# Moving the activation buffers by 32 bytes, and summing the norms' totals in two rounded halves

## The reference

```python
def rmsnorm_2(x, g):
    y = xf * lax.rsqrt(jnp.mean(xf * xf, axis=-1, keepdims=True) + EPS)
...
h = rmsnorm(x, norm_mix_g[layer])          # layer 0: RWKV time mix; layer 1: conformer convolution
x = x + memory_cross_attention(rmsnorm(x, norm_xattn_g[layer]), memn, ...)
x = x + conv_ffn(rmsnorm(x, norm_ffn_g[layer]), ffn_w_in[layer], ffn_dw[layer], ffn_w_out[layer])
...
# then one hybrid layer: gated linear attention + forgetting attention on rmsnorm_2(x) @ w_in,
# an output projection, and a feed-forward with 2 x 2816 inner features
```

## Time and profile before

| | |
|---|---|
| median of 3 runs | 2613.34 us (2609.92 to 2617.4) |
| span of the profiled execution | 2609.5 us |
| PE busy | 2513.7 us, 96% of the span |
| PEld busy | 2370.4 us, 91% |
| DVE, ACT, POOL busy | 1338.1, 1120.9, 995.1 us |
| matmuls at L565 (the dense products) | about 17,800 |

### The profile page before, as it was taken

How to read it: one execution, slowest core, us unless ns; L and a number is a source line. 1 busy time by engine, 2 the same in 40 slices (tenths; PEclk the granted TensorE clock), 3 DMA queues, 4 the chain that set the end, 5 groups by cost and what they waited for, 6 DMA issues and landing times.

```text
span 2609.5 us, 62290 instructions
## 1 busy us (share of the span) xinstructions
PE 2513.7 (96%) x25298; PEld 2370.4 (91%) x25298; DVE 1338.1 (51%) x2034; ACT 1120.9 (43%) x1649; POOL 995.1 (38%) x488
## 2 busy tenths in 40 slices
PE   6999898999999999998999999999999999999998
PEld 6888896897999999977989999999999769999998
DVE  7657554613477741798534777621153344455521
ACT  7844455544434433334534334433244443444432
POOL 3324220461444444325323444444442104444442
PEclk8899999999999999999999999999999999999999
DMA  4221001251222232313211222233222102222232
GB/s 147 74 65 58 2 1 63 94 181 41 89 96 96 88 101 101 130 65 105 89 65 65 97 96 96 97 105 113 89 89 74 41 1 94 97 92 96 94 100 73
DMA packets 62180, 219.43 MB, mean 84 GB/s; under 512 B 6752, under 2 KB 9184, under 8 KB 61408
## 3 DMA queue, kind: packets, MB, share of 16 engines
q1 hardware_dynamic: 58880, 207.76, 23.8%
q10 hardware_dynamic: 3168, 9.75, 1.1%
HBM read 213.29 MB, written 4.19 MB: 83 GB/s over the span
## 4 chain that ended last, share of the span: by engine, by line
PE 83%; DVE 8%; issue 6%; ACT 2%; POOL 1%; DMA 0%; DVEq 0%; POOLq 0%; ACTq 0%
PE psum L565 70%; DVE psum L2685 5%; PE psum L707 3%; PE psum L715 2%; PE psum L1066 1%; PE psum L1015 1%; PE psum L1245 1%; PE psum L1246 1%; POOL wl L514 1%; PE psum L1281 1%; DVE psum L2254 1%; ACT wh L1373 0%; PE psum L677 0%; PE psum L1269 0%; PE psum L684 0%
## 5 line engine op out<-in xcount | busy, mean ns | idle before, releaser
L514 POOL TENSOR_TENSOR wl<-raw,wh 128x1024 fp32r<-128x1024 f32 x388 | 949.0, 2456 | 1472.2 <-ACT wh L1373 1472.1
L565 PE MATMUL psum<-acth,wh 128*128 128x256 f32 x3792 | 763.4, 283 | 21.0 <-DVE actl L2776 8.2
L565 PE MATMUL psum<-actl,wh 128*128 128x256 f32 x3792 | 753.1, 280 | 0.0
L565 PE MATMUL psum<-acth,wl 128*128 128x256 f32 x3792 | 753.0, 280 | 0.0
L1373 ACT ACTIVATE wh<-raw 128x1024 fp32r<-128x1024 f32 x388 | 407.0, 1056 | 628.4 <-PE psum L565 610.9
L565 PEld LDWEIGHTS psum<-acth,wh 128*128 128x128 f32 x3792 | 582.1, 189 | 38.6 <-issue 30.4
L565 PEld LDWEIGHTS psum<-acth,wl 128*128 128x128 f32 x3792 | 581.0, 189 | 0.0
L565 PEld LDWEIGHTS psum<-actl,wh 128*128 128x128 f32 x3792 | 580.3, 189 | 0.0
L2615 DVE TENSOR_TENSOR cu<-psum,rstd 128x512 f32<-128x512 f32 x132 | 91.0, 689 | 241.7 <-PE psum L565 224.8
L565 PE MATMUL psum<-hidh,wh 128*128 128x256 f32 x1056 | 209.6, 276 | 0.0
L565 PE MATMUL psum<-hidh,wl 128*128 128x256 f32 x1056 | 209.3, 276 | 0.0
(11 more groups left out here) (436 smaller groups left out, 4044.3 us busy)
## 6 DMA issues: line engine op xcount, KB each, us to landing
raw<-in_weights SPq DMA_DIRECT2D x388, 512.0 KB, 3.3
xt<-in_x SPq DMA_DIRECT2D x4, 512.0 KB, 5.6
xt<-in_x ACTq DMA_DIRECT2D x1, 2048.0 KB, 9.2
out_x<-xt SPq DMA_DIRECT2D x6, 256.0 KB, 2.3
mem<-in_mem ACTq DMA_DIRECT2D x1, 1024.0 KB, 11.0
memn<-memh ACTq DMA_DIRECT2D x1, 1024.0 KB, 5.4
memn<-meml ACTq DMA_DIRECT2D x1, 1024.0 KB, 9.3
memh<-memn ACTq DMA_DIRECT2D x1, 1024.0 KB, 4.7
```

The source lines that it names most:

```text
L514: pool.tensor_tensor(wl[:, s, :], raw[:, s, :], wh[:, s, :].bitcast(F32), ALU.subtract).then_inc(split_done, 1)
L565: ins = pe.matmul(out[:, n:n + HALF], w, m[:, n:n + HALF], start=first and n == 0, stop=last and n + HALF >= out.shape[1])
```

## The change

1. `acth` is moved up by 32 bytes, so `acth` and `actl` begin 64 bytes beyond a multiple of 128. The small buffers behind are reordered so that `zone` stays where it was. The squares' buffer `sq` now begins 96 bytes beyond a multiple of 128, that is 32 beyond a multiple of 64.
2. Of a norm's sum ACT writes a rounded copy (`sum_high`, into `sums`, which lies on `sq`), DVE the rest (`sum_low`), and `norm_total` takes both with a rounded matrix of ones in matmuls of 256 columns: four for 512 tokens, two for 256. The first norm, the layer norm (`exact_total`) and `acc_x` in `in2` keep the float32 matmul.
3. `norm_total` stands one tile later in `up0`, `up1`, `up2`, `cin`, `in2`, `q1` and `o`; in `kv0` it stays. Loops are cut differently to suit.

```diff
         xt = place("xt", [P, KT, T + 1])
+        cursor[0] += 32
         act_at = cursor[0]
+        assert act_at % P == 64
...
-        common = place("common", [P, 3 * P])
+        par = place("par", [P, NPAR + 6])
+        sq = place("sq", [P, 2, T])
+        sums = at("sums", [P, 2, T], F32R, sq_at)
+        common = place("common", [P, 2 * P])
+        ones_r = place("ones", [P, P], F32R)
+        assert zone % 512 == 192 and sq_at % 64 == 32
...
+            def norm_total(stage, n=T, to=4):
+                pe.wait_ge(sum_lo, plan(stage, "sums") + 1)
+                for j in range(2):
+                    for c in range(0, n, HALF):
+                        ins = pe.matmul(bank[to][:, c:c + HALF], ones_r[:, :], sums[:, j, c:c + HALF], start=j == 0 and c == 0,
+                                        stop=j == 1 and c + HALF >= n)
+                ins.then_inc(sum_mm, 1)
...
                 tile("o", j, "post", acth, actl)
-                if j == 1:
+                if j == 2:
                     norm_total("norm_mem0", MEM)
...
             def ffn(l):
                 up, norm = f"up{l}", f"norm_ffn{l}"
                 tile(up, 0, norm, acth, actl)
+                tile(up, 1, norm, acth, actl)
                 norm_total(norm)
-                dense(up, norm, acth, actl, units=2 * FT - 4, skip=1)
+                dense(up, norm, acth, actl, units=2 * FT - 4, skip=2)
...
                 tile("cin", 0, "norm_conv", acth, actl)
+                tile("cin", 1, "norm_conv", acth, actl)
                 norm_total("norm_conv")
...
                 pe.matmul(bank[4][:, :], ones, acc_x[:, :], start=True, stop=True)
-                pe.matmul(bank[5][:, :], ones, acc_y[:, :], start=True, stop=True).then_inc(sum_mm, 1)
+                norm_total("norm_h", to=5)
...
+            def sum_high(stage, n=T):
+                act.wait_ge(sq_used, plan(stage, "sq") + KT + SC)
+                act.activation(sums[:, 0, 0:n], rstd[:, 0:n], ACT.Identity).then_inc(sum_hi, 1)
...
+            def sum_low(stage, n=T, of=rstd):
+                dve.wait_ge(sum_hi, plan(stage, "sums") + 1)
+                dve.tensor_tensor(sums[:, 1, 0:n], of[:, 0:n], sums[:, 0, 0:n].bitcast(F32), sub).then_inc(sum_lo, 1)
```

More of the change, by code:

```diff
@@ L165, in norm @@
         n = KT if split else 0
-        self.take(stage, sq=KT, rstd=1, split=n, val=n)
+        self.take(stage, sq=KT, rstd=1, split=n, val=n, sums=n // KT)
     def __call__(self, stage, what):
@@ L208, in build_program @@
         plan.take(f"down{l}", tile=8, x=KT)
-    plan.take("norm_h", sq=2 * KT, rstd=1, split=KT, val=KT, total=1)
+    plan.take("norm_h", sq=2 * KT, rstd=1, split=KT, val=KT, total=1, sums=1)
     plan.take("final", x=KT)
@@ L261, in build_program @@
         zone = cursor[0]
[L262 removed]
+        ident, blk64 = (common[:, j * P:(j + 1) * P] for j in range(2))
+        ones = ones_r[:, :].bitcast(F32)
+        assert zone % 512 == 192 and sq_at % 64 == 32
         b_eps, b_ln, b_gn, b_rn, b_q, b_eps2 = (eps[:, j:j + 1] for j in range(6))
@@ L603, in tile, with exact_total @@
                 ins.then_inc(units_used, 1)
-            def norm_total(stage, n=T):
+            def exact_total(stage):
                 pe.wait_ge(sq_used, plan(stage, "sq") + KT + SC)
-                pe.matmul(bank[4][:, 0:n], ones, rstd[:, 0:n], start=True, stop=True).then_inc(sum_mm, 1)
+                pe.matmul(bank[4][:, :], ones, rstd[:, :], start=True, stop=True).then_inc(sum_mm, 1)
+            def norm_total(stage, n=T, to=4):
[5 more added lines that the diff above has]
+                ins.then_inc(sum_mm, 1)
             def down(stage, source, hi, lo):
@@ L633, in _ @@
             pe.wait_ge(common_in, 16)
-            norm_total("norm0")
+            pe.wait_ge(ones_ready, 1)
+            exact_total("norm0")
             for b in (1, 2):
-                pe.matmul(bank[b][:, 0:3 * P], ones, common[:, :], start=True, stop=True)
-                pe.matmul(bank[b][:, 3 * P:T], ones, ident, start=True, stop=True)
+                for c in range(0, T, HALF):
+                    pe.matmul(bank[b][:, c:c + HALF], ones, common[:, :], start=c == 0, stop=c > 0)
             def mixed(stage, j, name):
@@ L1035, in attention @@
                     tile("q1", 0, "norm_x1", headh, headl)
+                    tile("q1", 1, "norm_x1", headh, headl)
                     pe.wait_ge(vt_ready, 8)
                     norm_total("norm_x1")
-                    dense("q1", "norm_x1", headh, headl, units=4, skip=1)
+                    for j in range(2, 5):
+                        tile("q1", j, "norm_x1", headh, headl)
                     pe.wait_ge(evacuated, plan("q1", "tile") + 2 + UC)
@@ L1099, in convolution @@
                 tile("cin", 0, "norm_conv", acth, actl)
+                tile("cin", 1, "norm_conv", acth, actl)
                 norm_total("norm_conv")
-                dense("cin", "norm_conv", acth, actl, units=4, skip=1)
-                for j in range(5, 8):
+                dense("cin", "norm_conv", acth, actl, units=4, skip=2)
+                for j in range(6, 8):
                     tile("cin", j, "norm_conv", acth, actl)
@@ L1123, in hybrid @@
                 tile("in2", 0, "norm_h", acth, actl)
+                tile("in2", 1, "norm_h", acth, actl)
                 pe.wait_ge(acc_ready, 1)
                 pe.matmul(bank[4][:, :], ones, acc_x[:, :], start=True, stop=True)
-                pe.matmul(bank[5][:, :], ones, acc_y[:, :], start=True, stop=True).then_inc(sum_mm, 1)
+                norm_total("norm_h", to=5)
                 def inner(skip, n):
                     dense("in2", "norm_h", acth, actl, units=n, skip=skip)
-                inner(1, 12)
+                inner(2, 8)
+                for j in range(10, 13):
+                    tile("in2", j, "norm_h", acth, actl)
                 pe.wait_ge(evacuated, t0 + 13 + UC)
@@ L1477, in deltas_normed @@
                         weight_high(UNIT0[stage] + (s + 1) * per - 1 + SLOTS, i, 4 * per)
+                if not gain:
+                    sum_high(norm)
             def last_deltas():
@@ L1955, in hybrid @@
             def hybrid():
+                act.wait_ge(acc_ready, 1)
+                act.activation(sums[:, 0, :], acc_y[:, :], ACT.Identity).then_inc(sum_hi, 1)
                 act.wait_ge(x_ready, plan("down1", "x") + KT + SC)
@@ L2207, in residual_normed @@
                             dve.tensor_tensor(b[:, :], b[:, :], sq[:, (n * s + j) % 2, :], add).then_inc(sq_used, 1)
+                if n == 1:
+                    sum_low(norm)
             def residual_last():
@@ L2651, in ffn @@
                                              op0=mul, op1=add).then_inc(acc_ready, 1)
+                    sum_low("norm_h", of=acc_y)
                 else:
```

24 lines of the change are left out of this document (14 added, 10 removed).

## The result

The changed kernel takes **2641.09 us** (median of four runs, 2640.94 to 2643.21) against 2611.63 us for the kernel before on the same chip: ratio 1.0115, 95% interval 1.0101 to 1.0129. It is slower by 1.2%, where 2581 us was forecast. The profiled execution has a span of 2639.1 us.

A forecast was written before the change was run, and what follows sets the result against it. PE's pace through the dense products was taken to bound the kernel. Pace -34.3, totals -1.6, `cin` +2.9, `o`/`kv0` +1.2 give -31.8 us: 2577.7 us span, plus 3.8 for the median, forecast 2581 us, range 2570 to 2602.

The forecast's parts named there:

- the three paces: Dense products: 113.2 ns on buffers 64 bytes beyond a multiple of 128, 116.6 on `acth`/`actl`, 117.8 on either kind.
- the 0.45 us of the total: Norm totals: four rounded matmuls take 0.45 us against 0.86, saving 0.4 us in each of `up0`, `up1`, `up2`, `q1`.
- the lateness in `cin`: Convolution: the total behind tile 1 delays the gate that starts DVE's chain; 2.9 us lost.
- the start of `acth`: Activation stages: `acth` 64 beyond a multiple of 128 runs at 113.2 ns, gaining 34.3 us, between 25 and 40.
- rival (b): New totals leave well placed buffers at 117.8 ns in stages behind them and down stages: +21 us, 2635 us; chance 0.09.
- The step on which I said the gain rests: New totals act like products on a buffer 32 bytes off, so well placed buffers behind them run at 113.2 ns.
- `o` and `kv0`: Two new copies and a queued `sum_high` delay the chain there; 1.2 us lost in all, between 0 and 2.4.
- the recurrence: Some operands move from 32 to 64 beyond a multiple of 128; nothing taken, within 1 us to either side.
- `sum_low`: DVE's copy of the norm sum's rest: 0.69 us, hidden under tile 0 in the up stages.
- Rival (c): `acth` keeps its pace whatever its start, for instance by where it lies against the weights: about 2617 us; chance 0.09.
- five other pairs in as many places: Argument that the start address sets the pace: five other buffer pairs reach 113.2 ns, all 64 beyond a multiple of 128.
- the pace term: Faster products in the activation stages: 4.5 or 3.4 ns gained per matmul, 34.3 us in sum.

The follow-up runs named there:

- the largest series: Small kernel of products alone, no reference work: 18 draws each at distances 32, 64, 112 and 192, behind float32 totals or own waits; 64 ran at 117.8 ns in all 18.
- the streams: Small kernels running only tiles of 128 x 256 products of ones, with varied operand starts and disturbances, none of the reference's work; measured as ns per matmul, 113.3 to 117.8 at 192.
- the kernel with `act` at 112: Kernel before with only the activation buffers moved, to 112 bytes beyond a multiple of 256, totals float32 at their old places: 2578.24 us, ratio 0.9879.

## Why the prediction was wrong

**Right:** that the stages are bound by a pace and not by waits; the three paces; the 0.45 us of the total; the lateness in `cin`. There the gate starts at 1077.45, 16.75 us behind the stage's first product at 1060.7, before 13.75 us (1065.15 from about 1051.4): 3.0 us later, where 2.9 were worked out. DVE's timeline there, as in the earlier trace rows:

```profile
1075.37 0.70 DVE L2711 TENSOR_TENSOR gp<-psum,rstd 128x512 f32<-128x512 f32 x1 [7.36 <-issue]
1075.98 0.68 DVE L2711 TENSOR_TENSOR glu<-psum,rstd 128x512 f32<-128x512 f32 x1
1077.45 0.76 DVE L2716 SCALAR_TENSOR_TENSOR gp<-gp,par,glu 128x512 f32<-128x512 f32 x1 [0.79 <-ACT glu L1900]
```

**The step that failed is "the start of `acth`":** "I take the well placed `acth` to run at 113.2 where it is not just behind a float32 matmul." The rows had shown 113.2 on buffers at 192 modulo 256 only; I wrote their class as "64 beyond a multiple of 128", which takes in 64 modulo 256, a place that no dense operand had. There a stream ran at 113.4 in few of its draws and at 117.8 in 18 of 18 in the largest series. That step alone turns -34.3 us into a loss: the run of the start alone is 23 us slower than the kernel before. (Of the 34.3 us, the four tiles of `q1`, 0.9 us, were never due to the start: `q1` works on `headh`, which doesn't move.)

**The same step hid a second loss.** I wrote that products on `acth` hand over to a well placed buffer at 113.2, from a trace in which `acth` stood at 32. With `acth` at 64, the three down stages and `out2` start at 117.8: (3168 + 384) x 4.5 = 16 us, 14.3 of them the price that rival (b) had for the down stages. It need not come out so: in the streams a handover from 64 at 117.8 to 192 was slow in four cases of eight.

**The step on which I said the gain rests**, that the new totals look like products on a buffer 32 bytes off and so are harmless, failed too: the totals with their later place cost 0.3% (the later place alone 0.15%, not clear of noise), since they took the stages at 32 from 116.7 to 117.8. Sized wrongly beside it: `o` and `kv0` together lost 2.7 us where 1.2 was taken and 2.4 was the bound; the recurrence lost 2.3 us where at most 1 was allowed; and `sum_low`, put at 0.69 us, has a median of 2.35 us in the kernel after, under a tile in the up stages, so that it cost nothing there:

```profile
L2215 DVE TENSOR_TENSOR sums<-rstd,sums x7: 424/2348/2360, 474.7 to 2258.9; 128x512 fp32r<-128x512 f32 x6, 128x256 fp32r<-128x256 f32 x1
```

Rival (b) has the outcome (2635 us) and its mechanism in part, yet not the place: `up1` was slow ahead of any total. Rival (c) named the right cause in its example, what `acth` lies against, the weights, though it forecast no change; and "five other pairs in as many places" was no evidence against it, for all five are at one distance. The sizes of the pace term were about right in themselves. With the start that does run at 113.3 (the kernel with `act` at 112), `up0` to `down0` gave 9.2 us where 9.1 was worked out, `up1` and `up2` 7.0 and 6.7 where 7.2 each, convolution and second attention 2.3 where 2.4, `in2` to `out2` 4.4 where 5.8. Ahead of `up0` it gave 9.0 where 2.7 was worked out, 1.7 of it because `xo0` ran fast this time, which is a matter of luck, and 2.9 ahead of `o`, which no run explains.

Not settled: why the pace depends on the distance, and what picks one of two paces; no run looks inside. Nor is it known why weights at 16 beyond 32 break the rule. And the nearest change to the one made was never run: `acth` at 192 modulo 256, the place at which the trace of before had shown 113.2.

## What to carry to other kernels

When a pace differs between buffers, name the property by the places that the trace has shown, modulo the largest power of two that fits them all, and count the untested residues: five buffers in one residue are one observation. Run a stream of the operation alone over all placements, in several draws each, before a layout is built on it; one small kernel here held the answer to this change. And an operand that carries one pace may be carrying that of the next stage too: price what follows a changed stage, not only the stage.

## What the runs showed of the hardware

- A matmul of 128 x 256 products (fp32r, weights loaded for each) takes 113.3 to 123.6 ns at the same granted clock of 1.00, depending on the starts of weights and moving operand modulo 256.
- At one placement there can be two stable paces (113.3 and 117.8 at distances 64 and 192, 116.7 and 117.8 at 32). Float32 matmuls, four products on another buffer, or a wait of 0.2 us can change one into the other but don't always, and the pace then holds for a whole stage, about 2000 products in the up stages.
- The best placement found is a moving operand at 112 modulo 256 with weights at 0: behind 5 to 13 slower products it ran at 113.3 in all 25 draws of the streams and in all three up stages of the kernel.
